# Two transformer blocks on one core: loads, weight splits and a norm moved at the seams

## The reference

```python
x1 = rmsnorm(h, norm1)
u, q, k, v, gates = split(x1 @ w_in)         # 1024, 1536, 1536, 1536, 2 x 1024 columns
pool = centred means of u by 4 windows, each group @ w_pool, times pool_scale
att = sum over 3 dilated groups of softmax(q k^T + bias) v      # 4 heads of 128
m = sigmoid(gate_a) * (pool @ w_a) + sigmoid(gate_b) * (att @ w_b)
h = h + m @ w_o
x2 = rmsnorm(h, norm2)
h = h + (gelu(conv(x2 @ w_up[:, :FF])) * (x2 @ w_up[:, FF:])) @ w_down
```

## Time and profile before

| | us |
|---|---|
| median of 3 runs | 2015.53 |
| lowest, highest | 2015.18, 2016.91 |
| the profiled execution | 2014.9 |
| its span | 2013.1 |
| busy: PE, PE weight loads | 1717.4 (85%), 1325.0 (66%) |
| busy: DVE, ACT, POOL | 868.9 (43%), 596.6 (30%), 114.8 (6%) |

### The profile page before, as it was taken

How to read it: one execution, slowest core, us unless ns; L and a number is a source line. 1 busy time by engine, 2 the same in 40 slices (tenths; PEclk the granted TensorE clock), 3 DMA queues, 4 the chain that set the end, 5 groups by cost and what they waited for, 6 DMA issues and landing times.

```text
span 2013.1 us, 32404 instructions
## 1 busy us (share of the span) xinstructions
PE 1717.4 (85%) x14363; PEld 1325.0 (66%) x14363; DVE 868.9 (43%) x1199; ACT 596.6 (30%) x761; POOL 114.8 (6%) x103
## 2 busy tenths in 40 slices
PE   6999899999899989999999998696987666666665
PEld 6999898998699988899757554486854222122221
DVE  3445556663443556566414735867623111011111
ACT  4345445443334434554321020333313010000100
POOL 0500000000140000000032400000000000000000
PEclk9999999999899999999989998798998888888888
DMA  8651366745675236686333110000085999999998
GB/s 283 220 180 64 126 225 230 273 182 176 227 257 175 79 127 231 243 299 226 128 52 126 42 47 6 2 3 2 4 309 198 409 409 410 410 409 410 410 410 328
DMA packets 154814, 419.94 MB, mean 209 GB/s; under 512 B 13906, under 2 KB 20749, under 8 KB 151618
## 3 DMA queue, kind: packets, MB, share of 16 engines
q1 hardware_dynamic: 154402, 417.87, 56.1%
q10 hardware_dynamic: 288, 0.22, 0.0%
HBM read 416.18 MB, written 1.89 MB: 208 GB/s over the span
## 4 chain that ended last, share of the span: by engine, by line
PE 58%; DMA 17%; DVE 10%; SPq 7%; ACT 5%; issue 3%; DVEq 0%; ACTq 0%
PE bank L1174 28%; DMA wring<-w_exp_up 8%; SPq L1083 7%; DMA R<-w_exp_down 4%; PE ps_s L1284 3%; PE ps_t L1284 3%; PE bank L1362 3%; PE bank L1337 3%; PE ps_s L1337 3%; ACT w_high L1774 2%; DVE w_low L2178 2%; PE ps_t L1344 1%; DMA wring<-w_in 1%; PE bank L1729 1%; DMA wring<-w_up 1%
## 5 line engine op out<-in xcount | busy, mean ns | idle before, releaser
L2178 DVE TENSOR_TENSOR w_low<-wring,w_high 128x2048 fp32r<-128x2048 f32 (+1 forms) x128 | 287.2, 2244 | 330.9 <-ACT w_high L1774 330.2
L1774 ACT ACTIVATE w_high<-wring 128x2048 fp32r<-128x2048 f32 (+1 forms) x128 | 238.1, 1860 | 359.0 <-PE bank L1174 304.5
L1174 PE MATMUL bank<-x_high,w_high 128*128 128x256 f32 x1600 | 325.6, 285 | 18.3 <-DVEq L2206 11.5
L1174 PE MATMUL bank<-x_low,w_high 128*128 128x256 f32 x1600 | 321.6, 283 | 0.0
L1174 PE MATMUL bank<-x_high,w_low 128*128 128x256 f32 x1600 | 319.6, 281 | 0.0
L1174 PEld LDWEIGHTS bank<-x_high,w_high 128*128 128x128 f32 x1600 | 247.2, 191 | 25.9 <-DVEq L2206 12.5
L1174 PEld LDWEIGHTS bank<-x_high,w_low 128*128 128x128 f32 x1600 | 247.7, 190 | 0.0
L1174 PEld LDWEIGHTS bank<-x_low,w_high 128*128 128x128 f32 x1600 | 246.7, 190 | 0.0
L1729 PE MATMUL bank<-R 128*32 128x512 f32 x512 | 69.5, 674 | 38.8 <-DMA R<-w_exp_up 27.7
L1729 PE MATMUL bank<-wring,R 128*32 128x512 f32 x512 | 70.3, 685 | 34.6 <-DMA wring<-w_exp_up 34.6
L2827 DVE TENSOR_TENSOR R<-bank,R 128x512 f32<-128x512 f32 x8 | 5.5, 692 | 202.6 <-PE bank L1729 202.6
(11 more groups left out here) (581 smaller groups left out, 2759.6 us busy)
## 6 DMA issues: line engine op xcount, KB each, us to landing
wring<-w_in SPq DMA_DIRECT2D x37, 2048.0 KB, 8.0
wring<-w_up SPq DMA_DIRECT2D x22, 2048.0 KB, 8.2
R<-w_exp_gate SPq DMA_DIRECT2D x16, 2048.0 KB, 23.4
wring<-w_exp_gate SPq DMA_DIRECT2D x16, 2048.0 KB, 23.9
R<-w_exp_up SPq DMA_DIRECT2D x16, 2048.0 KB, 23.6
wring<-w_exp_up SPq DMA_DIRECT2D x16, 2048.0 KB, 24.1
R<-w_exp_down SPq DMA_DIRECT2D x16, 2048.0 KB, 23.6
wring<-w_exp_down SPq DMA_DIRECT2D x16, 2048.0 KB, 24.0
```

The lines of the kernel that those rows point to most:

```text
L1174: mm = pe.matmul(b[:, i * S:(i + 1) * S], left, right, start=k == 0 and m == 0 and i == 0, stop=k == last and m == 2, skip_group_check=True)
L1774: a.activation(high_of(l, job), half_block(l, job, wring), ACT.Copy).then_inc(w_high_ready, 1)
L2178: v.tensor_tensor(half_block(l, job, w_low), half_block(l, job, wring), high_of(l, job).bitcast(F32), ALU.subtract).then_inc(w_low_ready, 1)
```

## The change

**Loads.** ada 4 goes in front of the last down block of layer 0, and ada 5 right behind it; they stood behind it both. They count as blocks of layer 0 now.

The diff:

```diff
--- before.py
+++ after.py
@@ -96,10 +96,14 @@
     for l in range(DEPTH):
         ahead = {("up", 0): (8 * l, 8 * l + 1), ("up", 3): (8 * l + 2,), ("up", 4): (8 * l + 3,)}
         if l:
-            ahead.update({("u", 0): (4, 5), ("q", 1): (6,), ("q", 2): (7,)})
+            ahead.update({("q", 1): (6,), ("q", 2): (7,)})
+        else:
+            ahead.update({("down", 5): (4,)})
         for name, j, _ in LAYER_BLOCKS:
             blocks += [(l, "ada", i) for i in ahead.get((name, j), ())]
             blocks.append((l, name, j))
+        if l == 0:
+            blocks.append((l, "ada", 5))
     return blocks
 
 
@@ -1207,6 +1211,8 @@
 
                 def pv(hh):
                     pe.wait_ge(probT_ready, l * 8 + 2 * hh + 2)
+                    if hh == 0:
+                        wait_emptied(pe, l, ("v", 5))
                     b = begin("pv", hh)
                     for g in range(NG):
                         hd = g * HEADS_PER_GROUP + hh
@@ -1218,7 +1224,7 @@
                 if l:
                     wait_emptied(pe, l - 1, ("down", 0))
                     for i in (4, 5):
-                        modulate(l, i)
+                        modulate(l - 1, i)
                 for j in range(4):
                     x_job("x1", j)
                 for name, n in (("u", 4), ("q", 6), ("k", 6)):
@@ -1236,7 +1242,6 @@
                             pe.wait_ge(cols_ready, 1)
                         wait_emptied(pe, l, ("k", 5))
                         scores(0)
-                wait_emptied(pe, l, ("v", 5))
 
                 for i in range(8):
                     if i:
@@ -1837,7 +1842,8 @@
                 for i in range(8):
                     softmax(i)
                     evac("gate", i, gate[:, 2 * i:2 * i + 2, :], ACT.Tanh, 0.5)
-                    high(l, SPLIT[("gate", i)] + 2)
+                    if i < 7:
+                        high(l, SPLIT[("gate", i)] + 2)
                     if i % 2 == 1 and i >= 3:
                         pv_high((i - 3) // 2)
                 for g in range(4):
@@ -1848,6 +1854,7 @@
                         ins = a.activation(x_high[:, k, :], b[:, kk * S:(kk + 1) * S], ACT.Copy,
                                            scale=cols[:, V_PS + k:V_PS + k + 1])
                     ins.then_inc(po_high_ready, 1)
+                high(l, SPLIT[("gate", 7)] + 2)
                 pv_high(3)
                 if l == 0:
                     a.wait_ge(csil_zero, 1)
@@ -1858,9 +1865,11 @@
                     high(l, SPLIT[("wa", j)] + 2)
                 for j in range(4):
                     wait_full(a, l, ("wb", j))
-                    high(l, SPLIT[("wb", j)] + 2)
+                    if j < 3:
+                        high(l, SPLIT[("wb", j)] + 2)
                     a.wait_ge(m_ready, 4 * l + j + 1)
                     a.activation(x_high[:, 2 * j:2 * j + 2, :], mT[:, 2 * j:2 * j + 2, :], ACT.Copy).then_inc(m_high_ready, 1)
+                high(l, SPLIT[("wb", 3)] + 2)
                 a.activation(stats[:, 24:25], stats[:, 25:26], ACT.Sqrt)
                 for j in range(4):
                     if j < 3:
@@ -1916,13 +1925,13 @@
 
 
 
-            for t in range(ST):
-                wait_emptied(a, DEPTH - 1, ("down", 2 * t + 1))
-                a.activation(junk2, h[:, t, :], ACT.Square, accum_out=st[:, t:t + 1]).then_inc(sumsq2, 1)
-                a.wait_ge(sumsq2, 2 * t + 3)
-                a.wait_ge(hn_ready, t + 1)
-                a.activation(junk2, xs[:, t, :], ACT.Square, accum_out=st[:, 2 + t:3 + t]).then_inc(sumsq2, 1)
-                a.wait_ge(sumsq2, 2 * t + 4)
+            for j in range(4):
+                t, c = j // 2, slice((j % 2) * 512, (j % 2 + 1) * 512)
+                wait_emptied(a, DEPTH - 1, ("down", j))
+                a.activation(junk2[:, 0:512], h[:, t, c], ACT.Square, accum_out=st[:, j:j + 1]).then_inc(sumsq2, 1)
+                a.wait_ge(hn_ready, j + 1)
+                a.activation(junk2[:, 512:1024], xs[:, t, c], ACT.Square, accum_out=st[:, 48 + j:49 + j]).then_inc(sumsq2, 1)
+                a.wait_ge(sumsq2, 2 * j + 4)
             a.wait_ge(ms2, 2)
             a.activation(st[:, 20:24], st[:, 16:20], ACT.Sqrt).then_inc(rms2, 1)
 
@@ -2080,7 +2089,7 @@
                 a.activation(yg[:, 0:512], h[:, t, half * 512:(half + 1) * 512], ACT.Square, accum_out=st[:, o:o + 1])\
                     .then_inc(sumsq2, 1)
                 take(("hx", j), h2T[:, 4 * half:4 * half + 4, t * P:(t + 1) * P], split=4)
-                a.wait_ge(sumsq2, 7 + j)
+                a.wait_ge(sumsq2, 11 + j)
             a.wait_ge(ms2, 3)
             a.activation(st[:, 28:30], st[:, 14:16], ACT.Sqrt).then_inc(rms2, 1)
             a.wait_ge(r3_ready, 1)
@@ -2257,7 +2266,8 @@
                     logits(i)
                     if i:
                         take_probT(i - 1)
-                    low(l, SPLIT[("gate", i)] + 2)
+                    if i < 7:
+                        low(l, SPLIT[("gate", i)] + 2)
                     if i % 2 == 0 and i >= 4:
                         pv_low((i - 4) // 2)
                 pv_low(2)
@@ -2273,6 +2283,7 @@
                     v.wait_ge(po_low_ready, 4 * l + g + 1)
                     v.nop().then_inc(dve_emptied, 1)
                 take_probT(7)
+                low(l, SPLIT[("gate", 7)] + 2)
                 pv_low(3)
 
                 def m_low(j):
@@ -2295,10 +2306,12 @@
                     wait_emptied(v, l, ("wb", j))
                     v.tensor_tensor(m, m, tmp, ALU.add).then_inc(m_ready, 1)
                     v.wait_ge(m_ready, 4 * l + j + 1)
-                    low(l, SPLIT[("wb", j)] + 2)
+                    if j < 3:
+                        low(l, SPLIT[("wb", j)] + 2)
                     if j:
                         m_low(j - 1)
                 m_low(3)
+                low(l, SPLIT[("wb", 3)] + 2)
                 for j in range(4):
                     wait_full(v, l, ("wo", j))
                     hv = h[:, :, j * HALF:(j + 1) * HALF]
@@ -2361,15 +2374,19 @@
                     wait_full(v, l, ("down", j))
                     hv = h[:, t, half * 512:(half + 1) * 512]
                     v.tensor_tensor(hv, down_bank[j], hv, ALU.add).then_inc(dve_emptied, 1)
+                    if l == DEPTH - 1:
+                        c = slice(half * 512, (half + 1) * 512)
+                        wait_emptied(v, l, ("down", j))
+                        v.tensor_tensor(xs[:, t, c], hv, normf[:, c], ALU.mult).then_inc(hn_ready, 1)
                 wait_emptied(v, l, ("down", 3))
                 v.memset(stats[:, 23:24], 0.0).then_inc(layer_done, 1)
 
 
-            for t in range(ST):
-                v.tensor_tensor(xs[:, t, :], h[:, t, :], normf, ALU.mult).then_inc(hn_ready, 1)
-            v.wait_ge(sumsq2, 6)
-            chain(v.tensor_scalar(st[:, 16:18], st[:, 0:2], 1.0 / D, EPS, ALU.mult, ALU.add))
-            chain(v.tensor_scalar(st[:, 18:20], st[:, 2:4], 1.0 / D, None, ALU.mult))
+            v.wait_ge(sumsq2, 10)
+            chain(v.tensor_tensor(st[:, 52:54], st[:, 0:4:2], st[:, 1:4:2], ALU.add))
+            chain(v.tensor_tensor(st[:, 54:56], st[:, 48:52:2], st[:, 49:52:2], ALU.add))
+            chain(v.tensor_scalar(st[:, 16:18], st[:, 52:54], 1.0 / D, EPS, ALU.mult, ALU.add))
+            chain(v.tensor_scalar(st[:, 18:20], st[:, 54:56], 1.0 / D, None, ALU.mult))
             v.scalar_tensor_tensor(st[:, 18:20], st[:, 16:18], EPS, st[:, 18:20], ALU.mult, ALU.add).then_inc(ms2, 1)
 
             def full_bank(job):
@@ -2384,11 +2401,11 @@
                         ins = v.tensor_scalar(dst(k), b[:, kk_ * S:(kk_ + 1) * S], mul(k), add(k), ALU.mult, ALU.add)
                     ins.then_inc(dve_emptied2, 1)
 
-            x2_evac("xc", lambda k: hT[:, k, S:T2], lambda k: mulT[:, 1, k:k + 1], lambda k: mod_col(1, 0, k))
             v.wait_ge(rms2, 2)
             chain(v.reciprocal(st[:, 24:28], st[:, 20:24]))
             for t in range(ST):
                 v.tensor_scalar(xs[:, t, :], xs[:, t, :], st[:, 26 + t:27 + t], None, ALU.mult).then_inc(xs2_ready, 1)
+            x2_evac("xc", lambda k: hT[:, k, S:T2], lambda k: mulT[:, 1, k:k + 1], lambda k: mod_col(1, 0, k))
             x2_evac("xl", lambda k: hT[:, k, 0:S], lambda k: mulT[:, 0, k:k + 1], lambda k: mod_col(0, 0, k))
             for t in range(ST):
                 chain(v.scalar_tensor_tensor(h[:, t, :], h[:, t, :], st[:, 24 + t:25 + t], normf, ALU.mult, ALU.mult))
@@ -2727,7 +2744,7 @@
                 chain(v.memset(order[:, i:i + 1], float(8 - i)))
             chain(v.memset(comb[:, :, N_EXP:], 0.0))
             chain(v.memset(posm[:, :, N_EXP:], 0.0))
-            v.wait_ge(sumsq2, 10)
+            v.wait_ge(sumsq2, 14)
             chain(v.tensor_reduce(st[:, 12:14], st[:, 40:44].rearrange("p (t c) -> p t c", t=ST), AX_X, ALU.add))
             v.tensor_scalar(st[:, 14:16], st[:, 12:14], 1.0 / D, EPS, ALU.mult, ALU.add).then_inc(ms2, 1)
             v.wait_ge(rms2, 3)
```

## The result

| | before | changed |
|---|---|---|
| median of 4 runs, us | 2015.55 | 1995.78 |
| lowest, highest | 2015.18, 2016.91 | 1995.26, 1999.23 |
| span of the profiled execution | 2013.1 | 1994.3 |
| mean granted clock of TensorE in it | 0.936 | 0.945 |

The ratio is 0.9903, 95% interval 0.9890 to 0.9915: 19.6 us faster (17.1 to 22.2). The forecast was 2000.8 with a range from 1996.8: faster, as predicted, but by 5.0 us more than forecast and 1.0 outside the range.

A forecast was written before the change was run, and what follows sets the result against it. Up to 1000 us TensorE is nearly always busy, so only its idle time can be won there. Terms 0 + 5.4 + 1.8 + 1.9 + 0 + 4.1 + 1.5 = 14.7 us off the 2015.5 median give 2000.8, range 1996.8 to 2005.5.

The forecast's parts named there:

- v5 to gate: Wait for v 5's banks moved to the first pv: TensorE's idle time only moves to the scores, term 0.
- Rival A: TensorE, not DVE's chain, paces the gate stage: the full 5.0 us come on top, 1995.8 us; chance 0.08.
- Tails of gate and wb: Splits of wa 1 and wo 1 moved back: 2 x 2.7 = 5.4 us before pv 3, 2 x 0.95 = 1.9 around wo.
- Layer seam: Modulation blocks' transfers moved between the layers: nothing on the critical path gets shorter, term 0.
- Second seam: Squares and products by quarters: TensorE turns the scaled x from 1005.75 instead of 1009.87, term 4.1 us.
- Its clock: Stretch at 1.2 GHz around pv 3 may stay or go with one gap left: 0 to 1.8 a layer, term 1.8.
- the 1.5 of the second seam: Full clock for x's transposes and first projections after a shorter gap: between 0 and 3.2 us, about half taken, 1.5.
- rival C: All the clock comes back, behind the gate stage and at the second seam: 18.2 us, 1997.3 us; chance 0.12.

The follow-up runs named there:

- the memsets: The changed kernel with five or eleven one-column memsets chained on DVE ahead of layer 0's first projection: 2000.68 us with five, 1998.25 us with eleven.

## Why the prediction was wrong by size

**v5 to gate, 0: right by order, not by clock.** The idle time moved to the scores, 0.87, 1.06 and 0.42 us in layer 1, 4.8 in all; the part alone gave nothing like 5.0, and when DVE's order was changed, the waits went. The prediction read off one trace that the gap at v5 was followed by no low stretch; in the other four traces with this gap there were six, at 1.4 us each. Rival A would have given almost exactly the measured time, for the wrong reason.

**Tails of gate and wb, 5.4 and 1.9: right.** 5.65 and 1.71 by the traces. The new 0.9 us wait of wo 1 for its low half stands in the table.

**Layer seam, 0: right**, by the part alone and by the change without it.

**Second seam, 4.1: right**, 4.37.

**The step that failed is "Its clock", and the 1.5 of the second seam.** By order 11.4 was forecast and 11.7 came; of the clock 3.3 was forecast and 7.5 came between the two profiled executions. At pv 3 the 1.8 was hit, though in another way than thought: all of it in layer 0 (2.86 us) and none in layer 1 (4.44), behind the same gap of 2.29 in both. At the second seam 2.8 came back instead of 1.5, within the bound of 3.2. The other 3.0 is the sum of places that the prediction put at nothing: the start (0.8), the two seams between wo and up (3.1), the layer seam (-0.9). Miss of the sum: 0.3 by order, 1.3 + 3.0 of clock, -0.4 unassigned, and 14.7 + 4.2 is the 18.8 of the spans, but for rounding.

The thought behind it was that a gap either is or isn't long enough to lower the clock, and that one trace shows which. The two traces of the changed kernel and the counts of pv 3 show that the same gap does both. The range should have carried that: every place with a stretch at 0.5 or next to a wait, whether edited or not, with some 1.6 us each to either side.

How much of it was luck? The first runs of the kernel before (2015.18 to 2016.91) hid the spread; in 53 further runs on three chips it went from 2011.34 to 2020.86. The changed kernel's second set, 1998.71, lies within the forecast's range; five ratios of kernels that differ by less than 1 us in their order of work (the changed one twice, without the transfers, and with the memsets) have a mean of 0.9915, 17.2 us. So some 2 us of the first result's 19.6 may be its own executions' luck, the start (0.8) among them, and without them the time would have been in the range, near rival C's. The other 5.5 beyond the order's 11.7 stay in the mean of five and have the size of the 5.8 that the counts give, so most of them look like a steady gain; one trace a kernel doesn't show them place by place. In the first pair of traces they only lay elsewhere: nothing at gate 0, where the kernel before happened to have no low stretch, and 1.55 at each seam between wo and up, where it had both.

## What to carry to other kernels

Before a wait is taken from one engine, list what the engine that ends the next wait does from one such wait to the next: if its step is the longer one, the idle time moves, and the gain is to be had by reordering that engine's own work (here a weight split behind the next logits, 6.8 us). Work that nobody is waiting for, but that itself waits for a transfer, must not stand ahead of a chain on the seam (7.4 us). And give the clock a term of its own: count each wait of TensorE, edited or not, as able to bring or lose a stretch at the lower level, here 1.1 to 1.6 us; read several traces of the kernel before to see how often each does, and repeat it in many runs before trusting a narrow range.

## What the runs showed of the hardware that I had not expected

One program on one core had its stretches at 1.2 GHz in different places from one execution to the next: 0.66 or 1.00 in 15 to 25 us, 0.91 or 1.00 at the seam of layer 0. The medians of the same kernel in two sets lay 2.9 us apart (1995.78 and 1998.71; ratios 0.9903 and 0.9909). Yet the places aren't free either: a wait of 2.29 us was followed by the full clock in layer 0 and by the lower one in layer 1 in all eight traces of the changed kernel and those built on it, and the waits of 2.48 us ahead of gate 0, which cost nothing by order, were followed by a low stretch in six of ten places, 1.4 us each.
